# Two experts in one pass: the second expert's block of 512 hidden columns moved from one block behind the first's to the same block

## The reference

```python
def moe_swiglu(h, w_router, b_router, w_gate_up, w_down):
    ...
    for e in range(N_EXPERTS):
        out = out + gates[:, e:e + 1] * swiglu(tok, w_gate_up[e], w_down[e])
```

## Time and profile before

| What | us |
|---|---|
| median of 3 runs (1621.73 to 1629.79) | 1627.89 |
| the profiled execution, its own time | 1627.29 |
| its span, first to last instruction | 1625.5 |
| TensorE busy in it | 1465.6 |
| VectorE busy | 657.2 |
| ScalarE busy | 504.6 |
| pass 1: first matmul, end of the scatter | 635.0, 874.4 |
| pass 2 | 883.2, 1126.6 |
| pass 3 | 1128.3, 1385.2 |
| pass 4 | 1385.2, 1613.1 |
| granule 9 issued in pass 1, in pass 2 | 679.73, 930.05 |
| split of half a granule, ScalarE (L969), VectorE (L1758) | 1.91, 2.29 |
| an issue of a granule to its landing, median (gate and up; down) | 16.2; 18.2 |

### The profile page before, as it was taken

The page is one execution under the profiler, slowest core; times in us unless marked ns, Lnnn a source line. Parts: engine busy times, 40 slices in busy tenths (PEclk is TensorE's granted clock), DMA queues, the critical chain, the costliest instruction groups (busy, mean ns, idle before and its releaser), DMA issues.

```text
span 1625.5 us, 25260 instructions
## 1 busy us (share of the span) xinstructions
PE 1465.6 (90%) x10834; PEld 1018.6 (63%) x10835; DVE 657.2 (40%) x731; ACT 504.6 (31%) x578; POOL 34.5 (2%) x66
## 2 busy tenths in 40 slices
PE   4999999999998895899997899999899999896887
PEld 2764788887775554677674677676666564563442
DVE  5933454444204444655531655453555530100002
ACT  2322534332203323444432445432444431000011
POOL 2001000000100010000000000000000000000000
PEclk9989999999999987999998999998899997798898
DMA  8686874454842052499999399999599999499991
GB/s 297 264 310 234 321 273 178 184 204 159 311 155 104 1 207 107 159 410 410 412 413 377 134 366 412 411 411 410 189 398 412 412 414 382 147 413 411 413 415 41
DMA packets 206828, 474.68 MB, mean 292 GB/s; under 512 B 9986, under 2 KB 10030, under 8 KB 206670
## 3 DMA queue, kind: packets, MB, share of 16 engines
q1 hardware_dynamic: 199968, 470.83, 74.6%
q10 hardware_dynamic: 6702, 1.71, 0.5%
HBM read 471.47 MB, written 1.05 MB: 291 GB/s over the span
## 4 chain that ended last, share of the span: by engine, by line
PE 73%; DMA 9%; SPq 7%; DVE 4%; issue 3%; ACT 2%; ACTq 1%; POOL 0%; DVEq 0%
PE ps L2193 33%; PE ps L2444 10%; SPq L481 7%; PE ps L2456 6%; DMA ring<-in_moe_w_down_dram 6%; PE ps L2276 4%; DMA ring<-in_ada_w_dram 2%; PE ps L2340 2%; PE ps L2169 2%; PE ps L2284 2%; PE ps L2004 1%; PE ps L2435 1%; PE ps L2434 1%; PE ps L2365 1%; DMA ring<-in_moe_w_gate_up_dram 1%
## 5 line engine op out<-in xcount | busy, mean ns | idle before, releaser
L1758 DVE TENSOR_TENSOR ring_lo<-ring,w 128x2048 fp32r<-128x2048 f32 x126 | 288.4, 2290 | 170.5 <-ACT w L969 131.7
L2444 PE MATMUL ps<-ring,arena 128*32 128x128 f32 (+1 forms) x4928 | 284.6, 317 | 55.3 <-issue 25.7
L969 ACT ACTIVATE w<-ring 128x2048 fp32r<-128x2048 f32 x126 | 240.5, 1912 | 229.9 <-PE ps L2193 229.9
L2444 PEld LDWEIGHTS ps<-ring,arena 128*32 128x32 f32 (+1 forms) x4928 | 202.7, 122 | 134.2 <-issue 70.2
L2193 PE MATMUL ps<-ring_lo,x_hi 128*128 128x512 f32 x560 | 220.3, 393 | 0.0
L2193 PE MATMUL ps<-w,x_hi 128*128 128x512 f32 x336 | 137.1, 408 | 3.2 <-DVE arena L1726 3.2
L2193 PE MATMUL ps<-w,x_lo 128*128 128x512 f32 x336 | 132.5, 394 | 0.0
L1434 DVE TENSOR_TENSOR ring_lo<-ring,w_hi 128x2048 fp32r<-128x2048 f32 x42 | 95.6, 2290 | 86.1 <-ACT w_hi L759 86.1
L2193 PEld LDWEIGHTS ps<-ring_lo,x_hi 128*128 128x128 f32 x560 | 106.4, 190 | 20.3
L759 ACT ACTIVATE w_hi<-ring 128x2048 fp32r<-128x2048 f32 x42 | 78.8, 1910 | 49.9 <-PE ps L2193 42.0
L2456 PE MATMUL ps<-ring,tri 128*32 128x512 f32 (+1 forms) x448 | 79.6, 614 | 13.1 <-DMA ring<-in_moe_w_down_dram 11.1
(11 more groups left out here) (381 smaller groups left out, 1630.3 us busy)
## 6 DMA issues: line engine op xcount, KB each, us to landing
ring<-in_moe_w_gate_up_dram SPq DMA_DIRECT2D x112, 2048.0 KB, 16.2
ring<-in_moe_w_down_dram SPq DMA_DIRECT2D x56, 2048.0 KB, 18.2
ring<-in_ada_w_dram SPq DMA_DIRECT2D x24, 2048.0 KB, 10.9
ring<-in_ffn_w_gate_up_dram SPq DMA_DIRECT2D x14, 2048.0 KB, 12.3
ring<-in_ffn_w_down_dram SPq DMA_DIRECT2D x7, 2048.0 KB, 7.7
ring<-in_sb_w_qkv_dram SPq DMA_DIRECT2D x6, 2048.0 KB, 8.5
ring<-in_s_w_out_dram SPq DMA_DIRECT2D x2, 2048.0 KB, 7.6
ring<-in_sb_w_out_dram SPq DMA_DIRECT2D x2, 2048.0 KB, 13.5
```

Of the source, the lines that this page charges most:

```text
L969: act.activation(half3(h).bitcast(F32R), ff_half(gran(pair_place(*main_granule(n))), half), ACT.Copy).then_inc(whi_done, 1)
L1758: dve.tensor_tensor(ff_half(ring_lo[place % RING][:, :], half).bitcast(F32R), ff_half(gran(place), half), half3(h), ALU.subtract).then_inc ...
L2444: ins = pe.matmul(dst[width * r:width * r + width, 0:cols], x[:, k, 0:width], weights[:, k, cols * r:cols * r + cols], start=k == 0, stop= ...
```

## The change

The change moves b's block f to a's block f. `pair_order` puts bg f, bu f and bd f among ag f+1, au f and ad f; the three engines issue b's block f, with its transpose and its down product, inside block f, and the end of the pass keeps only the results and the gather. ScalarE copies b's transposed block ahead of the split of the second half of ag f+1. At the very end TensorE waits once more for the last gathered tokens. No instruction on data is added or removed.

The diff, cut to its core (SyncE follows `pair_order`):

```diff
 def pair_order():
-    order = [("ag", 0), ("au", 0), ("ag", 1), ("au", 1), ("ad", 0), ("bg", 0), ("ad", 1), ("bu", 0), ("ag", 2)]
-    for f in range(2, FB):
-        order += [("au", f), ("bg", f - 1), ("ad", f), ("bu", f - 1)]
-        if f < FB - 1:
-            order += [("ag", f + 1)]
-        order += [("bd", f - 2)]
-    return order + [("bg", FB - 1), ("bu", FB - 1), ("bd", FB - 2), ("bd", FB - 1)]
+    order = [("ag", 0), ("au", 0), ("ag", 1), ("au", 1), ("ad", 0), ("bg", 0), ("bu", 0), ("bd", 0)]
+    for f in range(1, FB):
+        order += [("au", f)] if f > 1 else []
+        order += [("bg", f), ("ad", f), ("bu", f)]
+        order += [("ag", f + 1)] if f < FB - 1 else []
+        order += [("bd", f)]
+    return order
...
 # ScalarE, pair_wide
-                    if f:
-                        silu_second(p, f - 1, width)
+                    silu_second(p, f, width)
                     w_round(2 * n + 5)
...
                         silu_tail(f + 1)
+                    turned_second(p, f, width)
+                    if f < FB - 1:
                         w_round(2 * n + 7)
-                    if f:
-                        turned_second(p, f - 1, width)
-                    if f < FB - 1:
                         w_round(2 * n + 8)
...
 # ScalarE, pair_end
                 pair_out(p, light)
-                silu_second(p, FB - 1, width)
                 gathered_out(p + 1)
-                turned_second(p, FB - 1, width)
...
 # VectorE, pair_wide
                     w_rest(2 * n + 5)
-                    if f:
-                        product_second(p, f - 1, width)
+                    product_second(p, f, width)
                     dve.wait_ge(a3_done, split * FB + f + 1)
...
 # VectorE, pair_end
                 gathered_out(p + 1)
-                product_second(p, FB - 1, width)
                 wait_used2(dve, p, "bd", FB - 1)
...
 # TensorE, pair_end
-                second_in(p, "bg", FB - 1, width)
                 gather(p + 1)
-                second_in(p, "bu", FB - 1, width)
-                second_down(p, FB - 2, width)
-                second_turn(p, FB - 1, width)
-                second_down(p, FB - 1, width)
...
 # TensorE, pair_wide
                     main_gate(f)
                     tail_turn(f)
-                    if f:
-                        second_in(p, "bg", f - 1, width)
-                    else:
+                    if f == 0:
                         pair_weights(p)
+                    second_in(p, "bg", f, width)
                     tail_down(f)
                     main_up(f)
-                    if f:
-                        second_in(p, "bu", f - 1, width)
+                    second_in(p, "bu", f, width)
                     main_turn(f)
                     tail_in("ag", f + 1, TAIL_GATE, t_gate)
-                    if f > 1:
-                        second_down(p, f - 2, width)
+                    second_turn(p, f, width)
                     main_down(f)
-                    if f:
-                        second_turn(p, f - 1, width)
+                    second_down(p, f, width)
                 pair_end(p, width)
...
 # TensorE, pair_light
                     first_in("au", f)
-                    if f:
-                        second_in(p, "bg", f - 1, W2)
+                    second_in(p, "bg", f, W2)
                     first_turn(f)
-                    if f:
-                        second_in(p, "bu", f - 1, W2)
+                    second_in(p, "bu", f, W2)
                     first_down(f)
+                    second_turn(p, f, W2)
                     if f < FB - 1:
                         first_in("ag", f + 1)
-                    if f > 1:
-                        second_down(p, f - 2, W2)
-                    if f:
-                        second_turn(p, f - 1, W2)
+                    second_down(p, f, W2)
                 pair_end(p, W2)
...
 # TensorE, after the loop
+                pe.wait_ge(xe_act, 2 * PAIRS + 2)
+                pe.wait_ge(xe_dve, PAIRS + 1)
```

More of the change, by code:

```diff
@@ L1032, in pair_light @@
                 for f in range(FB):
-                    if f:
-                        silu_second(p, f - 1, W2)
+                    silu_second(p, f, W2)
                     act.wait_ge(m_tr, p * FB + f + 1)
@@ L1037, in pair_light @@
                     act.activation(dst, src, ACT.Copy).then_inc(m_aT, 1)
+                    turned_second(p, f, W2)
                     if f < FB - 1:
                         silu_first(f + 1)
-                    if f:
-                        turned_second(p, f - 1, W2)
                 pair_end(p, W2, True)
@@ L1822, in pair_light @@
                     product_first(f)
-                    if f:
-                        product_second(p, f - 1, W2)
+                    product_second(p, f, W2)
                 pair_end(p, W2, True)
```

## The result

The changed kernel took 1716.14 us in the median of 4 runs (1714.02 to 1718.38). The kernel before took 1628.84 us in 4 runs beside it (1621.73 to 1631.98). The ratio is 1.0543, with a 95% interval of 1.0505 to 1.0581. The forecast was 1692 us and the range 1664 to 1720. The sign, the main mechanism and the range held, the range by 4 us. Of the 91.1 us by which the profiled span grew (1625.5 to 1716.6), 64.7 were forecast, and 26 were not.

The account below looks back on a forecast made before the run. It took passes 1 and 2 as nearly bound by TensorE, pass 4 by transfers, pass 3 between. Pass terms +26.6, +26.3, -1.8 and +13.6 sum to 64.7 on 1627.3 us: forecast 1692 us, range 1664 to 1720.

Parts of the forecast that it names:

- The start: Pass 1, block 1: main gate 1 ends at 686.8, ad1 lands at 695.7 after some 7 us wait, main up 1 ends at 705.4.
- From granule 10 on the ring binds: Pass 1 after granule 10's issue: transfers bind, bd6 lands 167.1 us later at 872.5, the scatter ends at 901.0, +26.6.
- Pass 2: Same work as pass 1, with 1.5 us added for the low clock: 269.7 against 243.4 us, +26.3.
- The scatters of passes 3 and 4: Ends of passes 3 and 4: scatters of 12.0 and 13.4 us, within pass changes of -1.8 and +13.6.
- The bound of 21.3 us: Pass 3's scatter, other bound: it takes 21.3 us as before the change, +9.3.
- the forecast's own spread: Whole kernel: 1676 to 1704 us, from varied granule landings, ad1's landing, the low clock and pass 3's scatter.
- rival (1): Scatters directly behind the sparse gather stay at the low clock, 9.3 us for each of three passes: 1720 us; chance 0.12.
- Waits over 30 us in passes 1 and 2: Expected sign: TensorE waits over 30 us for transfers in each of passes 1 and 2, where it was 4.
- (2): TensorE waits in block 1, but the ring refills and only main up 1's delay is paid: 1666 us; chance 0.09.
- (3): ad1 and bu1 land in time; only the order on TensorE counts, 1 us a wide pass: 1630 us; chance 0.04.
- (4): ad1 and bu1 in time; ends' old waits, 1.9 a pass, and pass 3's slow scatter, 9.3, go: 1610 us; chance 0.03.

Follow-up runs that it names:

- e1: The changed kernel with granules listed in the order TensorE uses them and two instead of five loaded ahead: 1639.98 us, ratio 1.0088.
- e8: The changed kernel with AHEAD at 2 instead of 5, its order of granules kept: 1716.02 us, ratio 1.0548.
- e6: The changed kernel with granules in order of use, the gather ahead of bd6, and bg0 behind the tail's down product in block 0: 1609.47 us, ratio 0.9904.
- e9: The kernel before with VectorE's last copy ahead of the scatter cut into 32 pieces, bd6 left in place: 1670.27 us, ratio 1.0267.
- e3: The changed kernel with the tail's down product ahead of bg0 in block 0 alone: 1705.93 us, ratio 1.0482.
- e4: The kernel before with the gather moved behind bd6 on all three engines, b's blocks still one behind: 1660.2 us, ratio 1.0194.

## Why the prediction was right, and which step failed

**The start, right.** Main gate 1 was to end at 686.8; granule 9 went out at 687.49. ad1 was to land at 695.7, and its product begins at 696.29. Granule 10 was put at 705.4 and came at 706.75. bg0 gave the priced delay: main up 0 began at 662.1 for 661.0. bg0 began 0.9 us earlier than priced, but it and the tail's down product ran partly at the lower clock (3.64 and 2.63 us for 1.9 each).

**From granule 10 on the ring binds, right.** bd6 was to end 9.2 us behind a landing at 872.5, so at 881.7; the gather begins at 883.43, and 1.4 of the 1.7 us are granule 10's. This is the term that carries passes 1 and 2. e1 and e8 show its cause: with the order by use it is gone, with AHEAD alone nothing changes.

**Pass 2, right within 2.2 us, but by two errors that cancel in part.** Granule 10 left 76.0 us into the pass, not 72.6. The longest of the extra terms is the second part of the gather in block 0, 7.09 us where 4.28 had been, again at the lower clock. Against this 3.4 stands the 1.5 that had been added for the scatter's clock: the scatter took 11.9 us at 1.00.

**The scatters of passes 3 and 4, the step that failed.** "so I take 12.0" for pass 3 and 13.4 for pass 4. Up to the gather's end both passes came as forecast: 240.5 us behind the start of pass 3 for 241.7, and 226.5 behind that of pass 4 for 228.1. From there to the scatter's end it was 3.98 + 22.9 = 26.9 us for 13.5, and 1.59 + 22.9 = 24.5 for 13.4: 24.5 us in sum, nearly all of the 26 that are missing. The working had argued that nothing stands between gather and scatter any more. That was so in passes 1 and 2. In passes 3 and 4 a wait for which the profile shows no releaser stands there. The one of pass 3 was in the profile before too, 2.65 us ahead of the slow scatter, behind bd6, and I let it drop with bd6 gone. The bound of 21.3 us had been kept in the range; it was too low by 1.6 us and by the wait. Pass 4's scatter had no such bound, and should have. So the measured time lies outside the forecast's own spread of 1676 to 1704, and inside the range only because that was drawn out to rival (1) at 1720. Rival (1) had the effect, the low clock in the scatters, and its total came within 4 us. But it put it on three passes, without the wait, and its cause, a scatter right behind the gather, was there in passes 1 and 2 too, where the scatters took 11.9 us at 1.00. Its closer total is partly luck.

**Waits over 30 us in passes 1 and 2, wrong.** They were 23.8 in pass 1 and 23.2 in pass 2. The 28 us of pass 1 are 19.8 more waiting for transfers and 8.3 more busy time: part of the standing time was filled by products at the lower clock. In a kernel that waits for its ring the idle time alone tells too little; length less old length tells it.

**Rivals.** (2) wanted the ring to fill again; from 715 to 860 us the transfers ran without a gap at 411 GB/s, 5.1 us a granule, and still TensorE waited, so it fell. (3) and (4) wanted ad1 and bu1 on time; they came 7.0 and 7.9 us late. (4) asked for slots in time and for no cost of bg0. e6 meets both by its edits and lands at the 1610 that (4) gave, and as (4) had it the largest part is the slow scatter of pass 3. That the totals meet is partly luck: (4) gave each pass 1.9 us for its shorter end, and pass 1 of e6 is 0.8 longer than before. What spoke against (3) and (4), the order of the queue, was indeed what decided.

**The clock.** Pass 3's scatter had TensorE busy 22.89 of 22.9 us and stayed at 0.50 to its end; pass 4's did as well. By the Trainium skill ("TensorE: Matmul & The Clock Gate", Part 1) sustained activity releases the throttle; no scatter that began slow in these traces was released before its end. Elsewhere the traces agree with it: in pass 3 of the kernel before, bu6 behind the gather took 5.36 us for 3.67, and the product right behind it ran at the full clock again.

**Open.** What the waits without a releaser ahead of the scatters of passes 3 and 4 are was not found, nor what the 8.7 us behind pass 1 are. The loading of instructions is a rival that no run tested. In the kernel before the profile's instruction queues moved 9 packets during the scatter of pass 1 and 5 in the 8.8 us behind it; in e9 they moved 11 under the slow scatter and none in the 1.3 us behind it. But in the 2.65 us ahead of the scatter of pass 3 they moved none. Which work or which wait ahead lets the clock fall is bounded, not settled. In the twelve traces here there are 48 scatters. Behind waits of 0.88 to 1.03 us with bd6 ahead, all 21 ran at the full clock. Behind waits of 1.6 to 5.0 us all 17 ran slow, for most or all of their length. With the gather right ahead and no wait, the 8 in passes 1 and 2 of the changed kernel, e1, e3 and e8 ran at the full clock; the 2 of e4, whose bd6 had waited, did not. For other products this doesn't hold: e3's tail product, behind 3.3 us, ran at either clock.

## What to carry to other kernels

When work is moved between steps of a pipeline that is fed from a ring by one in-order queue, list the loads by first use again in the new order: a granule listed a block too early keeps its slot a block longer, and here everything behind it came late, 76 us for two granules a pass. Do the same for the kernel that you compare with: its list was worth 11 us too, most of what the repaired change seemed to win. A seam of a pass is to be priced with its clock: behind waits of 1.6 to 5.0 us, 12 us of products took up to 11 more. Price each repair alone and together; a sum that fits is worth no more than the spread of the runs in it.

## What was not expected of the hardware

A stretch of fp32 products that keeps TensorE busy throughout can stay at 1.2 GHz for 22.9 us (0.50 granted, 22.90 busy), nearly twice its 11.9 us, though nothing in it waits. And a wait of 5.0 us ahead of it instead of 0.9, made by a slower copy alone (e9), set this off in each of the three passes where the scatter had run at the full clock.
